# Three squares moved to ScalarE, low weights last and products of zeros ahead, in the first units of a float32 transformer kernel

## The reference, cut to what matters

```python
def rms_norm(x, g):
    y = xf * lax.rsqrt(jnp.mean(xf * xf, axis=-1, keepdims=True) + EPS)
    return (y * g.astype(jnp.float32)).astype(x.dtype)

def swiglu_ffn(h, w_gu, w_down):
    gate, up = jnp.split(h @ w_gu, 2, axis=-1)
    return (jax.nn.silu(gate) * up) @ w_down

x = x + 0.5 * swiglu_ffn(rms_norm(x, norm_g[i, 0]), ffn_w_gu[i, 0], ffn_w_down[i, 0])
```

## Time and profile before

| what | value |
|---|---|
| median of 3 timed runs | 2300.97 us (2299.47 to 2302.4) |
| the profiled execution's own time | 2295.68 us |
| its span, first to last instruction | 2293.9 us |
| mean granted TensorE clock in the span | 0.994 |
| TensorE busy | 2239.7 us, 98% of the span |
| VectorE, ScalarE, GpSimd busy | 1270.2, 905.5, 154.3 us |
| read from memory | 213.66 MB, 96 GB/s over the span |

### The profile page before, as it was taken

The page is one execution under the profiler, slowest core; times in us unless marked ns, Lnnn a source line. Parts: engine busy times, 40 slices in busy tenths (PEclk is TensorE's granted clock), DMA queues, the critical chain, the costliest instruction groups (busy, mean ns, idle before and its releaser), DMA issues.

```text
span 2293.9 us, 24761 instructions
## 1 busy us (share of the span) xinstructions
PE 2239.7 (98%) x9874; PEld 1794.0 (78%) x9874; DVE 1270.2 (55%) x1970; ACT 905.5 (39%) x1402; POOL 154.3 (7%) x127
## 2 busy tenths in 40 slices
PE   7999999899899999999999999999899999999999
PEld 6888887766677888888888887777688888877777
DVE  6443445877754434455433445777566535655863
ACT  4222333555433322233322334777533222236672
POOL 2000002000040000020000012000040000020000
PEclk9999999999999999999999999999999999999999
DMA  5323224021123323223223224222045343331220
GB/s 188 101 83 110 97 69 149 19 92 56 35 78 127 114 92 110 83 100 112 83 83 128 78 69 145 72 72 90 19 129 165 120 138 114 103 129 52 77 74 37
DMA packets 201746, 217.39 MB, mean 95 GB/s; under 512 B 4968, under 2 KB 194536, under 8 KB 201632
## 3 DMA queue, kind: packets, MB, share of 16 engines
q1 hardware_dynamic: 194960, 193.48, 26.0%
q0 software_dynamic: 6528, 22.26, 2.9%
q10 hardware_dynamic: 144, 0.08, 0.0%
HBM read 213.66 MB, written 6.32 MB: 96 GB/s over the span
## 4 chain that ended last, share of the span: by engine, by line
PE 88%; DVE 6%; ACT 3%; issue 2%; DMA 0%; SPq 0%; DVEq 0%; ACTq 0%
PE ps L1581 87%; PE ps L1585 1%; DVE sb_wlo L1050 1%; ACT sb_whi L613 1%; DVE sb_gla_at L1302 1%; DVE sb_gla_ek L1287 1%; ACT sb_xh L613 0%; DMA sb_raw<-ffn_w_gu 0%; DVE sb_gla_eq L1290 0%; DVE sb_xl L1055 0%; DVE sb_gla_xb L1282 0%; DVE sb_gla_d L1269 0%; ACT sb_hyb_th L613 0%; DVE sb_gla_on L1213 0%; DVE sb_gla_vt L1196 0%
## 5 line engine op out<-in xcount | busy, mean ns | idle before, releaser
L1581 PE MATMUL ps<-sb_xh,sb_whi 128*128 128x512 f32 x2120 | 847.8, 400 | 22.7 <-DVE sb_xl L1055 10.3
L1581 PE MATMUL ps<-sb_xh,sb_wlo 128*128 128x512 f32 x2120 | 830.6, 392 | 0.0
L1581 PE MATMUL ps<-sb_xl,sb_whi 128*128 128x512 f32 x2120 | 829.9, 391 | 0.0
L1050 DVE TENSOR_TENSOR sb_wlo<-sb_raw,sb_whi 128x1024 fp32r<-128x1024 f32 (+2 forms) x401 | 474.1, 1187 | 517.2 <-ACT sb_whi L613 516.0
L613 ACT ACTIVATE sb_whi<-sb_raw 128x1024 fp32r<-128x1024 f32 (+2 forms) x401 | 387.0, 968 | 597.3 <-PE ps L1581 588.9
L1581 PEld LDWEIGHTS ps<-sb_xh,sb_whi 128*128 128x128 f32 x2120 | 401.1, 189 | 117.0 <-issue 25.1
L1581 PEld LDWEIGHTS ps<-sb_xl,sb_whi 128*128 128x128 f32 x2120 | 401.2, 189 | 86.6 <-issue 6.0
L1581 PEld LDWEIGHTS ps<-sb_xh,sb_wlo 128*128 128x128 f32 x2120 | 400.6, 189 | 85.6
L1581 PE MATMUL ps<-sb_ffn_ah,sb_whi 128*128 128x512 f32 x704 | 277.6, 394 | 0.0
L1581 PE MATMUL ps<-sb_ffn_ah,sb_wlo 128*128 128x512 f32 x704 | 276.0, 392 | 0.0
L1581 PE MATMUL ps<-sb_ffn_al,sb_whi 128*128 128x512 f32 x704 | 273.3, 388 | 0.0
(11 more groups left out here) (249 smaller groups left out, 1762.1 us busy)
## 6 DMA issues: line engine op xcount, KB each, us to landing
sb_raw<-ffn_w_gu SPq DMA_DIRECT2D x86, 1024.0 KB, 5.1
sb_raw<-ffn_w_down SPq DMA_DIRECT2D x32, 1024.0 KB, 4.9
sb_raw<-gla_w_in SPq DMA_DIRECT2D x12, 1024.0 KB, 5.3
sb_raw<-diff_w_in SPq DMA_DIRECT2D x12, 1024.0 KB, 5.1
sb_ada_raw<-w_ada POOLq DMA_DIRECT2D x12, 1024.0 KB, 6.2
sb_raw<-w_in SPq DMA_DIRECT2D x10, 1024.0 KB, 5.2
sb_raw<-ffn_w_down SPq DMA_DIRECT2D x16, 512.0 KB, 3.5
sb_raw<-ffn_w_down SPq DMA_DIRECT2D x16, 256.0 KB, 2.6
```

What stands on the lines that cost most here:

```text
L1050: e.tensor_tensor(lo, raw[panel % NRAW][:, 0:nk, off:off + 128], hi.bitcast(F32), ALU.subtract).then_inc(sem["w_lo"], 1)
L1581: return e.matmul(out, lhsT, rhs, start=start, stop=stop, skip_group_check=skip)
```

## The change

It does four things, all at the start of the program.

- ScalarE squares x's tiles 5, 6 and 7 in place of VectorE, one after each of the copies of units 1, 2 and 3. They go to `rb`, `lnb` and a buffer of the first feed-forward network (`ub[1]`). VectorE only adds them, in two instructions on a new semaphore `sq_add`.
- VectorE makes `wlo` of units 1, 2 and 3 ahead of those two sums.
- Units 0 to 3 run by a new function `first_rows`: for each tile the two products with high weights, and behind all eight tiles the eight products with low weights. Its waits are spread: `whi` at the start, each tile's `xh` and `xl` ahead of the product that reads it, `wlo` ahead of the last eight.
- VectorE's program begins with a memset of `lnb` to zero, and TensorE's with five products of that buffer by itself in full float32, into a bank that nothing else uses then. ScalarE waits for the last of the five (it is to write `lnb`) before its copy of unit 1.

The title of the change also speaks of paired heads of the third mixer; they are as they were.

```diff
 SEMS = """
-x_hi x_lo sq sq_first sq_last norm lnb
+x_hi x_lo sq sq_first sq_add sq_last norm lnb warm
+        first_squares = rb[:, :], lnb[:, :], ffn_mem[0][3][1][:, :]
@@ ScalarE's program
-            w_hi(2 - NSLOT)
+            w.wait_ge(sem["warm"], 2)
+            for u, (part, m) in enumerate(zip(first_squares, (5, 6, 7))):
+                w_hi(u + 2 - NSLOT)
+                act(part, x[:, m, :], ACT.Square).then_inc(sem["sq_first"], 1)
@@ VectorE's program
+            e.memset(lnb[:, :], 0.0).then_inc(sem["warm"], 1)
             w.wait_ge(sem["par"], 16)
             w_lo(1 - NSLOT)
             for m in range(KT):
                 x_lo(0, m)
-            w_lo(2 - NSLOT)
-            e.tensor_tensor(rb[:, :], x[:, 5, :], x[:, 5, :], ALU.mult).then_inc(sem["sq_first"], 1)
-            for k, m in enumerate((6, 7)):
-                w.wait_ge(sem["sq_first"], 2 * k + 1)
-                e.tensor_tensor(lnb[:, :], x[:, m, :], x[:, m, :], ALU.mult).then_inc(sem["sq_first"], 1)
-                w.wait_ge(sem["sq_first"], 2 * k + 2)
-                e.tensor_tensor(rb[:, :], rb[:, :], lnb[:, :], ALU.add).then_inc(sem["sq_first"], 1)
+            w_lo(4 - NSLOT)
+            for k in (1, 2):
+                w.wait_ge(sem["sq_first"], k + 1)
+                w.wait_ge(sem["sq_add"], k - 1)
+                e.tensor_tensor(rb[:, :], rb[:, :], first_squares[k], ALU.add).then_inc(sem["sq_add"], 1)
@@ TensorE's program
+            def first_rows(u, bank):
+                w.wait_ge(sem["w_hi"], u + 1)
+                for t in range(KT):
+                    if u == 0:
+                        w.wait_ge(sem["x_hi"], t + 1)
+                    mm(psum[bank][:, :], whi[u][:, t, :], XH[t], t == 0, False)
+                    w.wait_ge(sem["x_lo"], t + 1)
+                    mm(psum[bank][:, :], whi[u][:, t, :], XL[t], False, False)
+                lo_done(w, u)
+                for t in range(KT):
+                    ins = mm(psum[bank][:, :], wlo[u][:, t, :], XH[t], False, t == KT - 1)
+                ins.then_inc(sem["w_used"], 1)
@@ norm_sums
-                    w.wait_ge(sem["sq_first"], 5)
+                    w.wait_ge(sem["sq_add"], 2)
@@ ffn
-                            rows(u, 0, KT, FFN_RING[p % 6], XH, XL, ("x_lo", 8 * NORM_OF_FFN[f]), True, True)
+                            if u < 4:
+                                first_rows(u, FFN_RING[p])
+                            else:
+                                rows(u, 0, KT, FFN_RING[p % 6], XH, XL, ("x_lo", 8 * NORM_OF_FFN[f]), True, True)
@@ the end of TensorE's definitions, ahead of ffn(0)
+            w.wait_ge(sem["warm"], 1)
+            for _ in range(5):
+                ins = mm(psum[FFN_AUX][:, :], lnb[:, 0:128], lnb[:, :], True, True)
+            ins.then_inc(sem["warm"], 1)
```

## The result

| | before | changed |
|---|---|---|
| median of 12 timed runs | 2300.43 us | 2293.65 us |
| lowest and highest | 2297.16, 2302.4 | 2292.74, 2296.92 |
| profiled execution, its own time | 2295.68 us | 2293.28 us |
| span, mean granted clock | 2293.9 us, 0.994 | 2291.5 us, 0.992 |

The changed kernel takes 0.9975 of the time of before, 95% interval 0.9966 to 0.9983: 5.8 us less, 3.9 to 7.8 (the medians alone are 6.8 us apart). The two profiled executions, though, are only 2.4 us apart. Both numbers need an explanation.

What follows compares the result with a forecast made beforehand. TensorE, busy 98%, was taken as the bound, with its start held up by the wait for `wlo2`. 1.15 + 3.52 + 0.11 = 4.78 us off the median 2300.97 gave 2296.2 us, range 2294 to 2298.3 (8 in 10: 2292 to 2300.5).

Steps and rivals of the forecast that it cites:

- What bounds the kernel: Whole kernel: TensorE busy 98%; at the start it waits 3.4 us for `wlo2`, behind five VectorE instructions on squares.
- The start's 4.78 us: Units 0 to 2: unit 2's second product starts at 21.07 instead of 25.85 us, 4.78 us sooner.
- the slack: GpSimd's sums, ending at 28.6, ahead of the product with ones at 31.7: 3.1 us left of 7.9.
- The terms: Start: 1.15 us from unit 1's earlier end, 3.52 from the wait that goes, 0.11 from the slow restart.
- 3.52 us: TensorE's wait for `wlo2` ahead of unit 2, from 21.99 to 25.51, goes: 3.52 us.
- the term of 1.15 us: Unit 1 ends at 20.84 instead of 21.99 us, said to need the full clock in unit 0.
- The cost of the order in unit 0: Unit 0: holding the eight low products back costs 1.36 us; with three products per tile it would end at 14.03.
- The slow products vary: Start: the number of slow products differs between runs; the 1.15 us would stay the same in the changed kernel.
- Zeros don't lift the clock: Rival, start: real products stay slow for 5.2 us more; gain 2.5 us, 2298.5 us; chance 8%.
- The clock falls in unit 0: Rival, unit 0 paced by `xl`: a half-pace stretch loses 1.6 us; gain 3.2 us, 2297.8 us; chance 8%.
- The clock falls more often in the mixers: Rival, mixers' waits: falls of 1.6 us each, six more give 4.8 us slower, 2305.8 us; chance 6%.
- Nothing arrives: Rival, rest of kernel: gain given back by two or three clock falls or a fixed wait, 2301 us; chance 5%.

Runs made afterwards that it cites:

- before again: The kernel before, unchanged, profiled a second time: products with ones at 37.97 us instead of 36.52, span 2296.8 us.
- the nine zeros' run: The changed kernel with nine products of zeros instead of five: products with ones at 33.15 us instead of 31.53, span 2290.9 us.

## Why the prediction was right, point by point

**What bounds the kernel.** Right. The start has the wait for `wlo2` behind five VectorE instructions, and all that moved from unit 4 on is a shift, but for the clock's falls. One reading behind it was loose: the forecast called 9 products in 3.4 us and 12 in 5.2 the same density, which is 0.38 and 0.43 us each. The start's 0.43 us is rather to be held against the rows at clock 0.50 behind the wait in the run with the zeros alone, 0.42 us apart, and it agrees.

**The start's 4.78 us.** Right in sum: 4.99 us by the two profiles (4.66 counted from the end of `xl`), with the zeros' begin and end, `xl`'s pace, `wlo2`, the squares in ScalarE's idle time and the loads all within some tenths. GpSimd's sums came 1.3 us later than I had them, which took half of the slack and no time.

**The terms.** Here the prediction went wrong without its sum showing it. It gave 3.52 us to moving the squares, 1.15 us to "the full clock in unit 0" and nothing to the order but a cost of 1.36 us in unit 0. By the marks, and in brackets counted from the end of `xl`, each part alone and each taken away from the whole, one profile each:

| part | gain alone, on before | loss when taken from the changed kernel |
|---|---|---|
| squares on ScalarE | 2.6 us (3.8) | 1.4 us (1.1) |
| new order | 3.8 us (3.5) | 0.7 us (0.2) |
| zeros | -2.3 us (-2.3) | 0.1 us (0.0) |

The 3.52 us hold for the squares as a single edit, with before's order around them. But the squares and the order are two cures for one wait, so either brings most of the gain and the second little; a sum over edits had no room for that. The step that failed is the term of 1.15 us and its condition, "which need the full clock in unit 0": without the zeros, and so at half pace until 12.02, the changed kernel loses 0.1 us, and an estimated half a microsecond with x as late as in its own profile. The zeros bring little or nothing to this order. I had taken the old order's unit 0, at half pace from 8.63, as what the zeros replace, though I had written down that the new order starts on `xh` alone: TensorE begins at 7.25, and sixteen products are light enough to catch `xl` up, just. Either brings these 1.15 us: the new order without the full clock, or the full clock in the old order (the zeros are worth 1.3 us there). So the sum came out right with a wrong condition on one of its terms, and that it did so is luck: the timeline needed unit 0 to keep `xl`'s pace, and the new order does this, just, at half pace too.

**The cost of the order in unit 0.** Right: 1.36 us forecast, 1.45 us by the mark (1.30 counted from the end of `xl`) when unit 0 alone goes back. That is the version to prefer, and in it the zeros do pay, 1.3 us.

**The slow products vary.** The clock's rise was a draw: from the rows, the full pace comes 5.2 us behind the first product before, 4.8 us in before again (13.22 - 8.44), 4.8 us without zeros (12.02 - 7.25) and 3.1 us in unit 0's old order without zeros. That the zeros ended as late as 8.10, near the forecast's 8.3, is part of the same draw. The Trainium skill ("TensorE: Matmul & The Clock Gate", What you observe) has the point of the rise move from run to run, and before's two traces agree, with 5.2 and 4.8 us and twelve and eleven slow products; that by it the end of unit 1 would be the same is true in the changed kernel, since `xl` sets it.

**The rivals.** *Zeros don't lift the clock* is refuted: in the changed kernel the real products start at 8.73 and 8.96, 0.23 us apart, and in the nine zeros' run real products are 0.23 us apart from the second on, with nothing but zeros ahead. *The clock falls in unit 0*: it did not. *The clock falls more often in the mixers*: the mechanism is real, and it did fall more often in the profiled execution, which is why the two profiles are 2.4 and not 5.0 us apart. I had put its price at 1.6 us for 3.4 us at half clock; the table gives 2.6 us for some 9 us more, 1 us for each 3.4, and the timed runs 1.5 us for each 0.001 of the clock, 1.1 us for each 3.4. Part of such a stretch lying over waits would explain it; in the dense start a fall did cost 1.6. But it comes and goes between executions of one kernel, and in the timed runs it went the other way: before's mean clock is the lower one. *Nothing arrives*: no.

**Where the last microsecond of the 5.8 comes from.** By the timed runs' own clocks, from the clock: at equal clock the kernels are 4.3 us apart, which agrees with the start's 4.7 to 5.0, and the rest goes with before's lower clock. The sum took before's first profile as the rule for its start. The second profile shows that in some executions the clock falls behind the wait for `wlo2` and the start takes 1.6 us more; the changed kernel has no such wait. That is one cause, and its share is open: how often the fall happens in timed runs was not measured, and one in every execution would lower the mean clock by 0.0007 (half of 3.4 us over 2297), a little over half of the 0.0013 by which the means differ. What is left of it lies behind the start, where the instructions are the same; chance is not ruled out there, and neither is the moment at which each kernel reaches the mixers' waits.

## What to carry to other kernels

- Before summing the gains of edits, ask for each whether it removes the same wait as another. Here two of three did, and the third, alone, gained nothing.
- Reaching a fixed wait sooner is worth nothing: the wait grows by what was won. Here the clock fell at that wait when it was 4.18 and 3.54 us long and not when it was 3.36, one execution each, which is too few for a rule. Shorten the wait first.
- Where TensorE must wait a microsecond or two in an otherwise dense program, products with an unused result are worth trying: seven such places gave 7.3 us here, about as much as all the work on the start (7.9 us by the same medians, unit 0 in the old order).

## What the runs showed of the hardware that was not expected

- Products of zeros lift the clock: behind 6.6 us of nothing but zeros the real products came 0.23 us apart from the second on.
- In the changed kernel the clock fell around a wait of 1.80 us in the first mixer; in before's first execution it stayed up around the same wait of 1.80 us. It stayed up once through a wait of 3.36 us in before's start and fell once behind one of 3.54 us in the same kernel. The length of the wait alone did not decide it in these rows.
- GpSimd's addition of 128x512 float32 took 1.6 us in some places and 2.15 us in others of one execution.
- The column of the granted clock reads 1.00 at the very start, while the products' distance is 0.43 us as at 0.50 elsewhere. At the start only the distance tells the clock.
- A memset of 128x512 float32 took VectorE 0.48 us, and five full-float32 products of 512 columns with the rise of the clock among them 6.6 us.
